# Cumulated gate rows copied by DMA instead of multiplied by ones, in a gated delta-rule kernel

## What is computed

```python
beta = jax.nn.sigmoid(b)
g = -jnp.exp(a_log) * jax.nn.softplus(a + dt_bias)
...
gc = jnp.cumsum(g, -1)
diff = gc[..., :, None] - gc[..., None, :]
decay = jnp.where(lower, jnp.exp(jnp.where(lower, diff, 0.0)), 0.0)
L = jnp.where(strict, jnp.einsum('bhnid,bhnjd->bhnij', kb, k) * decay, 0.0)
sol = lax.linalg.triangular_solve(L + jnp.eye(C), rhs, left_side=True, lower=True, unit_diagonal=True)
```

## Time and profile before

| | us |
|---|---|
| Median of 3 runs | 3025.56 (3021.94 to 3032.6) |
| The profiled execution | 3026.43, its span 3024.8 |
| TensorE busy | 2846.9, 94% of the span |
| VectorE busy | 1986.5, 66% |
| ScalarE busy | 1217.2, 40% |
| GpSimd busy | 896.9, 30% |

### The profile page before, as it was taken

One profiled execution on the slowest core, in us unless ns is written; L12 is line 12 of the kernel. 1 busy time (PEld: TensorE's weight loads), 2 busy tenths in 40 slices (PEclk: granted clock), 3 DMA queues, 4 the chain that ended last, 5 costly groups with the idle time before them and its releaser, 6 DMA issues.

```text
span 3024.8 us, 54010 instructions
## 1 busy us (share of the span) xinstructions
PE 2846.9 (94%) x21277; PEld 2699.6 (89%) x21277; DVE 1986.5 (66%) x2407; ACT 1217.2 (40%) x1496; POOL 896.9 (30%) x576
## 2 busy tenths in 40 slices
PE   3779999999999799999999999969999999999998
PEld 3779999999999687899999999969988989999996
DVE  6756656656666656765665666676789888745454
ACT  2143553553553534443333333334333333533343
POOL 3555655665665642000000000000445544000000
PEclk7889999999999999999999999989999999999999
DMA  9746556556555446555555555535444544555554
GB/s 332 279 137 196 187 173 198 183 180 196 189 175 195 145 168 208 208 183 187 187 180 188 186 183 187 185 125 167 155 148 159 161 147 155 179 183 186 181 204 147
DMA packets 285852, 552.90 MB, mean 183 GB/s; under 512 B 18881, under 2 KB 56306, under 8 KB 284530
## 3 DMA queue, kind: packets, MB, share of 16 engines
q1 hardware_dynamic: 266482, 474.81, 49.3%
q0 software_dynamic: 19200, 75.54, 6.6%
HBM read 548.19 MB, written 2.10 MB: 182 GB/s over the span
## 4 chain that ended last, share of the span: by engine, by line
PE 81%; DVE 11%; issue 3%; ACT 3%; POOL 1%; DMA 1%; SPq 0%; DVEq 0%; ACTq 0%; POOLq 0%
PE pg L989 31%; PE pg L767 15%; PE pd L1002 10%; PE pd L989 6%; PE pg L1002 3%; PE pd L878 3%; PE pd L891 2%; PE pd L714 2%; DVE wl L1822 1%; PE pg L788 1%; DVE arena L1597 1%; POOL wl L575 1%; DVE arena L2101 1%; DVE arena L2131 1%; PE pd L837 1%
## 5 line engine op out<-in xcount | busy, mean ns | idle before, releaser
L1822 DVE TENSOR_TENSOR wl<-wr,wh 128x1024 fp32r<-128x1024 f32 x616 | 769.4, 1260 | 553.1 <-ACT wh L1385 551.6
L1385 ACT ACTIVATE wh<-wr 128x1024 fp32r<-128x1024 f32 x616 | 652.4, 1060 | 1032.0 <-PE pg L989 667.2
L989 PE MATMUL pg<-hh,wh 128*128 128x256 f32 x2944 | 839.3, 285 | 19.1 <-issue 8.3
L989 PE MATMUL pg<-hl,wh 128*128 128x256 f32 x2944 | 835.1, 284 | 0.0
L989 PE MATMUL pg<-hh,wl 128*128 128x256 f32 x2944 | 834.6, 283 | 0.0
L575 POOL TENSOR_TENSOR wl<-wr,wh 128x1024 fp32r<-128x1024 f32 x216 | 555.7, 2578 | 457.3 <-ACT wh L1214 456.6
L989 PEld LDWEIGHTS pg<-hh,wh 128*128 128x128 f32 x2944 | 566.5, 192 | 33.3 <-issue 21.7
L989 PEld LDWEIGHTS pg<-hl,wh 128*128 128x128 f32 x2944 | 566.5, 192 | 0.5
L989 PEld LDWEIGHTS pg<-hh,wl 128*128 128x128 f32 x2944 | 566.6, 192 | 0.0
L1214 ACT ACTIVATE wh<-wr 128x1024 fp32r<-128x1024 f32 x216 | 227.8, 1057 | 545.6 <-PE pg L767 435.5
L767 PE MATMUL pg<-hh,wh 128*128 128x256 f32 x1472 | 432.1, 294 | 14.2 <-POOL wl L575 13.1
(11 more groups left out here) (357 smaller groups left out, 4577.9 us busy)
## 6 DMA issues: line engine op xcount, KB each, us to landing
wr<-in_w_in SPq DMA_DIRECT2D x224, 512.0 KB, 3.9
wr<-in_ffn_w_gu SPq DMA_DIRECT2D x176, 512.0 KB, 4.2
wr<-in_gdn_w_in SPq DMA_DIRECT2D x128, 512.0 KB, 3.9
arena<-in_mod_w POOLq DMA_DIRECT2D x64, 1024.0 KB, 6.7
wr<-in_ffn_w_down SPq DMA_DIRECT2D x88, 512.0 KB, 4.5
arena<-in_mod_w SPq DMA_DIRECT2D x32, 1024.0 KB, 8.0
wr<-in_gdn_w_in SPq DMA_DIRECT2D x128, 256.0 KB, 2.9
wr<-in_gdn_w_out SPq DMA_DIRECT2D x56, 512.0 KB, 4.5
```

What stands on the lines that cost most here:

```text
L989: m = nc.tensor.matmul(bank[:, n * T:(n + 1) * T], w[s][:, k, n * P:(n + 1) * P], act[x][:, k0 + k, :], skip_group_check=True, start=(firs ...
L1385: a(wh[c % 4][:], wraw[c % 4], ACT.Copy).then_inc(s_hc, 1)
L1822: v.tensor_tensor(wl[c % 4][:], wraw[c % 4], wh[c % 4][:].bitcast(F32), ALU.subtract).then_inc(s_lc, 1)
```

## The change

Three edits go together.

- GpSimd writes the cumulated gates (32 heads by 256 tokens) once to a DRAM scratch `gate_rows`. For each turn two DMAs from GpSimd's queue read the four heads' rows back with a stride of zero over the partitions, straight into the SBUF tile `rowb`. The first pair is started before turn 0, each later pair in the turn before, behind the `low` of chunk 9. `rowm`, GpSimd's product L604 and TensorE's product L843 go.
- VectorE takes dt's rows from `rowb` in SBUF instead of from PSUM, and its order at the turn is dt, qkn, taps instead of taps, qkn, dt.
- TensorE's loop over six turns is written out.

```diff
-VO = order("scal", "qkn", "dt", "lt", "u2", "at", ...
+VO = order("dt", "qkn", "scal", "lt", "u2", "at", ...
-        rowm = take(2, VH, P)
+        rowb = take(2, VH, P)
+        gate_rows = nc.dram_tensor("gate_rows", (NH, T), F32).ap()
...
+            def row_load(it):
+                rows = gate_rows.rearrange("h (c t) -> c h t", c=TT)[:, bass.ds(it * VH, VH), :]
+                for c in range(TT):
+                    pool.dma_start(rowb[:, c], rows[c].unsqueeze(0).broadcast_to([P, VH, P])).then_inc(s_row, 16)
             def batch(it, o_low=None):
-                restart()
-                rows = gcT[0:NH].rearrange("p (c t) -> p c t", c=TT).unsqueeze(2).broadcast_to([NH, TT, VH, P])
-                pick = ident[0:NH, bass.ds(it * VH, VH)].unsqueeze(1).unsqueeze(3).broadcast_to([NH, TT, VH, P])
-                nc.gpsimd.tensor_tensor(rowm[0:NH], rows, pick, ALU.mult).then_inc(s_g, 1)
...
                     low(it + 1, t + 2)
+                    if t == 7 and not o_low:
+                        pool.wait_ge(s_v, it * len(VO) + VO["dt"])
+                        row_load(it + 1)
...
             pool.wait_ge(s_p0, 13)
+            pool.wait_ge(s_v0, V0["gc"])
+            pool.dma_start(gate_rows, gcT[0:NH]).then_inc(s_rw, 16)
+            pool.wait_ge(s_rw, 16)
+            row_load(0)
             pool.wait_ge(s_v0, V0["tok"])
...
-                pe.wait_ge(s_g, bg + GO["rowm"])
-                for n in range(2):
-                    m = nc.tensor.matmul(pd[1][:, n * 512:(n + 1) * 512], ones[0:NH, :],
-                                         rowm[0:NH, n].rearrange("p a b -> p (a b)"), start=True, stop=True)
-                m.then_inc(s_pe, 1)
...
-                V("dt")
...
-            with pe.Fori(0, NIT - 2) as j:
+            for j in range(NIT - 2):
                 beside(delta(j), lambda c: gchunk(j + 1, c))
                 gchunk(j + 2, 0)
...
                 link(v.tensor_copy(tkc, tk[:, :, bass.ds(it * VH, VH)]))
+                dve.wait_ge(s_row, it * 32 + 32)
+                for c in range(TT):
+                    for h in range(VH):
+                        n = c * VH + h
+                        m = stt(out=dTb[:, n, :], in0=rowb[:, c, h], scalar=tkc[:, c, h:h + 1], in1=mneg[:],
+                                op0=ALU.subtract, op1=ALU.min)
+                done(m)
+                Ac("rn")
+                done(v.tensor_tensor(qk.rearrange("p a b -> p (a b)"), qk.rearrange("p a b -> p (a b)"), rnb, ALU.mult))
                 if mods:
                     done(taps(it + 1))
                 else:
+                    dve.wait_ge(s_v, bv + VO["qkn"])
                     dve.sem_inc(s_v, 1)
-                Ac("rn")
-                done(v.tensor_tensor(qk.rearrange("p a b -> p (a b)"), qk.rearrange("p a b -> p (a b)"), rnb, ALU.mult))
-                PEw("rows")
-                for c in range(TT):
-                    for h in range(VH):
-                        n = c * VH + h
-                        m = stt(out=dTb[:, n, :], in0=pd[1][:, n * P:(n + 1) * P], scalar=tkc[:, c, h:h + 1], in1=mneg[:],
-                                op0=ALU.subtract, op1=ALU.min)
-                done(m)
```

More of the change, by code:

```diff
@@ L48, in order @@
     return {n: i + 1 for i, n in enumerate(names)}
-PEO = order("ssq", "rows", "vtok", "gram", "ktok", "t2", "x2", "tx2", "u2", "x4", "tx4", "u4", "x8",
+PEO = order("ssq", "vtok", "gram", "ktok", "t2", "x2", "tx2", "u2", "x4", "tx4", "u4", "x8",
             "tx8", "u8", "x16", "tx16", "u16", "x32", "tx32", "u32", "x64", "ux64", "v0", "s", "o0", "r",
             "qs", "v1", "o1", "mod", "otr")
-VO = order("scal", "qkn", "dt", "lt", "u2", "at", *[f"{a}{s}" for s in LEVELS for a in ("x", "t")],
+VO = order("dt", "qkn", "scal", "lt", "u2", "at", *[f"{a}{s}" for s in LEVELS for a in ("x", "t")],
            "x64", "u64", "o0", "rhs1", "o1", "on", "modt", "og")
@@ L57 @@
            "rstd", "qkv", "z")
-GO = order("rowm")
 LN_QSCALE = -0.5 * math.log(128.0)
@@ L337, in build @@
         s_a = sem("s_a")
-        s_g = sem("s_g")
+        s_rw = sem("s_rw")
+        s_row = sem("s_row")
         s_cst = sem("s_cst")
@@ L679, in tables, with wide_load @@
                 tt(s, s, tb_, ALU.add).then_inc(s_tab, 1)
-            def row_load(dst, src, sem):
+            def wide_load(dst, src, sem):
                 pool.dma_start(dst, src.unsqueeze(0).broadcast_to([P, D])).then_inc(sem, 16)
             pool.wait_ge(s_ck, CK_FF + 4)
-            row_load(g_row, A["ln_g"][0, 0], s_bc)
-            row_load(b_row, A["ln_b"][0, 0], s_bc)
-            row_load(g2_row, A["ln_g"][0, 1], s_bd)
+            wide_load(g_row, A["ln_g"][0, 0], s_bc)
+            wide_load(b_row, A["ln_b"][0, 0], s_bc)
+            wide_load(g2_row, A["ln_g"][0, 1], s_bd)
             pool.wait_ge(s_ev, 4)
-            row_load(b2_row, A["ln_b"][0, 1], s_bd)
+            wide_load(b2_row, A["ln_b"][0, 1], s_bd)
             pool.wait_ge(s_vp, 2)
@@ L706, in _ @@
             pool.wait_ge(s_ck, CK_LAST + 8 + 4)
-            row_load(fg_row, A["final_g_2"], s_be)
+            wide_load(fg_row, A["final_g_2"], s_be)
         @block.tensor
@@ L827, in delta @@
             def delta(it):
-                bp, bv, ba, bg = it * len(PEO), it * len(VO), it * len(AO), it * len(GO)
+                bp, bv, ba = it * len(PEO), it * len(VO), it * len(AO)
                 def V(name): pe.wait_ge(s_v, bv + VO[name])
```

## The result

| | before | changed |
|---|---|---|
| Median, us | 3025.56 (3021.94 to 3035.83) | 3052.17 (3050.2 to 3053.29) |
| Profiled execution's span | 3024.8 | 3050.4 |
| S of turn 1, turn 6, turn 7 | 319.97, 886.46, 1007.97 | 325.95, 911.14, 1034.11 |

The changed kernel is slower: its time is 1.0082 times that before (95% interval 1.0065 to 1.0098), 26.6 us. Forecast were 3050 and a range of 2999 to 3057. All of it arises up to turn 7; behind it the changed kernel makes good 0.5 us.

A forecast was written before the change was run, and what follows sets the result against it. TensorE bounds the kernel, 81% of the chain of waits. Five turns +9.0, turn 6 +1.3, clock +11.5, turn 0 +5 and turn 7 -2 sum to +24.8 us: 3050, range 2999 to 3057, the likeliest case's own 3036 to 3058.

The forecast's parts named there:

- The jump's price and ssq behind sqb: TensorE at the turn: the loop's jump costs some 1.3 us ahead of turns 1 to 5; written out, it goes.
- dt hidden: VectorE at the turn: dt from SBUF ends by about 5.1 us after sqb, before rn at 5.4, costing nothing.
- `mods` and the low parts start together: VectorE and GpSimd, both about 7.4 us after sqb's end: they hold each other up; t2 comes at 24.7.
- The collision as the cause: Ahead of t2: VectorE instructions held by GpSimd's low parts make t2 5.4 us later than TensorE could; chance 0.56.
- first rival: No collision, the whole gain: `mods` get through, t2 19.3 us after sqb in turns 1 to 6; -27 us, 2998; chance 0.22.
- Five turns: From sqb's end in turn 1 to that in turn 6: 575.5 us instead of 566.5, +9.0 before the clock's part.
- The clock's term: TensorE behind the stall ahead of t2: a lower clock costs 1.65 us in turns 0 to 6, +11.5 in all.
- Turn 0: Rows by DMA may land 2 us late or not at all, on top of the collision: +5 us, bounds +2 and +8.
- Turn 6: From sqb's end to t2: 24.7 us instead of 23.4, +1.3 before the clock's part.
- Turn 7 and behind: Turn 7: sqb 2 us shorter without L604, but `mods` meet a longer GpSimd train; -2 us, bounds -5 and +3.
- Worse: Rival: VectorE held through several products on end, or copies late in each turn; beyond 3058 us, chance 0.05.
- The jump only: Rival: writing out the loop leaves the 1.3 us; TensorE waits that much less at t2, little change; no chance given.

The follow-up runs named there:

- narrow `mods`: The changed kernel with the four `mods` instructions of a turn's first slot cut from 512 to 32 columns; 3004.68 us, ratio 0.9928.
- moving one half and its loads: The changed kernel with one first-slot `mods` half moved later, row transfers behind chunk 14's low part, and later modulation loads; 2996.61 us, ratio 0.9904.
- run without waits: Not named outright; 109.55 and 19.12 are both given for the changed kernel with first-slot `mods` cut to 32 columns; 3004.68 us, ratio 0.9928.
- order alone: The kernel before with only VectorE's order changed to dt, qkn, taps, product rows and TensorE's loop kept; 3023.3 us, ratio 0.9984.
- loop alone: The kernel before with only TensorE's loop of six turns written out; 3017.8 us, ratio 0.9969.
- run with late row transfers: The changed kernel with one first-slot `mods` half moved later and the row transfers started behind chunk 14's low part, not chunk 9's; 3017.59 us, ratio 0.9971.

## Why the prediction was right, step by step

- **The jump's price and ssq behind sqb**: right. TensorE's 1.3 us went, ssq starts at S + 0.06 in turns 0 to 6.
- **dt hidden**: right. It took 4.34 us beside a low part and ended at S + 4.57; at most S + 5.1 was foreseen.
- **`mods` and the low parts start together**: right to 0.3 us, and so were the ends: lt at S + 16.7 and 18.85 (17 and 19.1), u1's end at 21.4 (21.2), u2's at 24.65 (24.7). One detail differs. Of the four instructions the first three were held, among them L1633, which I had not counted; low 6 came at S + 12.7 rather than 13.8, and the last L1635 ran free behind it. So the three L1635 took 2.1 us in the mean, where 2.5 was named. The trace of before had a sign that one input in SBUF is enough: there L1661, a copy of 128x8, was held until GpSimd's low part of chunk 3 ended at 325.60.

```profile
321.90 3.74 DVE L1661 COPY arena<-vc 128x8 f32 x1
```

- **The collision as the cause**: shown, by the narrow `mods` (turns of 109.55 us, where the first rival said 109.7) and by moving one half and its loads.
- **Five turns**: +17.25 forecast, clock included, +18.7 measured. The clock's term was 1.65 a turn; t2 to the next S is 92.3 us in the mean (585.19 / 5 - 24.7) against 90.43 in the run without waits (109.55 - 19.12), so 1.9, and 1.4 to 2.7 by turn. The fall of the earlier trace rows is no support for this term: in turn 2 of before TensorE had idled only some 1.7 us, for the jump, and the clock fell all the same, which it did not in turns 1 and 3 to 5. The earlier trace rows carries it.
- **Turn 0**: +8.1 from S to S, where +5 and 1.65 were forecast, but its S came 2.1 us earlier; at S of turn 1 the loss is 6.0. The 2.1 us are luck: S of turn 0 lies between 200.4 and 206.7 in the fourteen traces, at 204.4 and 204.6 in the order alone and the loop alone, whose code ahead of it is that of before, and before's own 206.7 is the latest. Rows late and collision add up there: t2 waited 7.2 us.
- **Turn 6**: from S to the start of turn 7's sqb it takes 119.57 us instead of 115.61, so +3.96, where +2.95 was forecast: t2 came 1.3 us later, as forecast, and the clock's part is 2.7 instead of 1.65. From S to S it is only +1.45, because the shorter sqb of turn 7 falls into it.
- **Turn 7 and behind**: from the start of its sqb to the end -3.0 (sqb 2.5 shorter, and the 0.5 behind it), where -2 was forecast. The parts so miss by +1.5 us (five turns), +1.4 (turn 0), +1.0 (turn 6) and -1.0 (turn 7), and the early S of turn 0 takes off 2.1: that the sum came within 1 us of +24.8 is in part luck, the mechanism is not.
- **Slips in the working**: the parts' own bounds add up to 3033 and 3061, not to 3036 and 3058; the time lies inside both. In turn 6 of before L575 ended 2.24 us behind L1731, not 2.38. Nothing else hangs on either.
- **"Worse", VectorE held through several products on end**, had been given 0.05 although the trace of before shows it: in turn 7 one L1630 was held for 12.37 us, and the stall of the earlier trace rows follows from it. In the changed kernel L1635 is held as long there, so it takes no part in the difference.

```profile
1035.16 12.37 DVE L1630 SCALAR_TENSOR_TENSOR arena<-arena,condt 128x512 f32<-128x512 f32 x1
1047.57 1.22 DVE L1743 TENSOR_TENSOR arena<-pd,masks 128x1024 f32<-128x1024 f32 x1
```

- **The jump only** was reasoned wrongly. I had TensorE wait 1.3 us less at t2 if the jump stayed. Kept, it moved t2 from S + 24.7 to 26.1 in turn 3: the norms, exp, the low parts and `mods` all stand behind ssq. The forecast didn't rest on it.
- **What the prediction didn't see**: that three edits which each look like work saved depend on each other, and that code ahead of a loop changes its jumps.

## What to carry to other kernels

Before taking 2 us off the engine that bounds, lay the steps of two engines that hold each other up on one time line, relative to the turn's start, and ask which pairs now begin together; here it went with 7 us a turn (111.7 against 118.7) whether two VectorE instructions met a gap of 2 to 2.8 us between two GpSimd products. When a piece of work is moved, follow every wait that counts it: the half moved to a later slot held up a load, and the load a train of low parts. And compare a stage that no edit touches as well: its change is a finding, not noise.

## What the runs showed of the hardware

- A VectorE instruction can be held through several GpSimd products on end: 7.84 us for one of 0.78 us, and 12.37 in turn 7 of before. A short one is held too: 128x32 for 2.44 us.
- The one-input L1633 (TENSOR_SCALAR, 128x512), 0.49 us when free, was held as well: 2.69 us.
- An issue of a transfer on GpSimd between products (0.77 us each) prolonged the hold: 1.5 us for two.
- Behind waits of 5.4 us TensorE ran 8 transposes in 1.97 us instead of 1.04; behind 1.92 us in 1.83 in turn 1 of the run with late row transfers, but behind the same wait in 1.09 in its turns 2, 4 and 5.
- The same loop stalls for up to 3.1 us at a jump or not at all, by where it stands in TensorE's code; its passes take 109 to 114 us with the stall and 105.4 to 107 without.
